# Root-mean-square norms: sums in four column tiles of PE, root and reciprocal on a quarter of the columns, spread back into PSUM by four products

## The reference

```python
def rms_norm(x, g):
    y = xf * lax.rsqrt(jnp.mean(xf * xf, axis=-1, keepdims=True) + RMS_EPS)
    return (y * g.astype(jnp.float32)).astype(x.dtype)
...
a_lat = modulate(rms_norm(h_lat, g_pre_t), sh_t, sc_t)      # before the mixer
h_lat = h_lat + gt_t * rms_norm(y_lat, g_post_t)            # residual behind it
f_lat_in = modulate(rms_norm(h_lat, g_pre_f), sh_f, sc_f)   # before the channels
h_lat = h_lat + gt_f * rms_norm(f_lat, g_post_f)            # residual behind them
```

## Time and profile before

| | |
|---|---|
| median of 3 runs | 2568.89 us (2568.54 to 2573.36) |
| the profiled execution | 2565.24 us, its span 2563.4 us |
| PE busy | 2413.9 us, 94% of the span |
| DVE busy | 1755.0 us, 68% |
| ACT busy | 1385.1 us, 54% |
| mean granted PE clock | 0.968 |

### The profile page before, as it was taken

The page is one execution under the profiler, slowest core; times in us unless marked ns, Lnnn a source line. Parts: engine busy times, 40 slices in busy tenths (PEclk is TensorE's granted clock), DMA queues, the critical chain, the costliest instruction groups (busy, mean ns, idle before and its releaser), DMA issues.

```text
span 2563.4 us, 32159 instructions
## 1 busy us (share of the span) xinstructions
PE 2413.9 (94%) x12058; PEld 1946.4 (76%) x12058; DVE 1755.0 (68%) x1806; ACT 1385.1 (54%) x1455; POOL 46.1 (2%) x87
## 2 busy tenths in 40 slices
PE   6989999998999997877988999999999999999997
PEld 3757778875787884756886788888888888888886
DVE  3569753426333334778655989898889888888886
ACT  3366343333222222565545677777777777777775
POOL 0001000001000000000000000000000000000000
PEclk8989999999999998988998999999999999999998
DMA  7245223345434333313462889999999999989894
GB/s 269 76 131 186 66 91 105 109 157 190 139 107 140 99 100 114 99 42 103 148 236 99 335 351 368 351 366 350 367 342 369 356 361 352 364 343 373 339 373 178
DMA packets 104679, 579.36 MB, mean 226 GB/s; under 512 B 11920, under 2 KB 13840, under 8 KB 54800
## 3 DMA queue, kind: packets, MB, share of 16 engines
q1 hardware_dynamic: 93072, 536.21, 56.8%
q0 software_dynamic: 11520, 41.95, 4.7%
HBM read 577.06 MB, written 1.05 MB: 226 GB/s over the span
## 4 chain that ended last, share of the span: by engine, by line
PE 85%; DVE 9%; ACT 3%; issue 1%; DMA 1%; SPq 0%; DVEq 0%; ACTq 0%
PE bank L616 25%; PE bank L618 25%; PE bank L617 25%; DVE cacc L1534 2%; PE bank L679 2%; PE bank L986 1%; PE bank L778 1%; DVE rstd L1475 1%; PE bank L1051 1%; PE bank L798 1%; DVE t L1490 1%; PE bank L654 1%; DVE al L1496 1%; DVE wlo L1455 1%; DMA mod_s<-in_mod 1%
## 5 line engine op out<-in xcount | busy, mean ns | idle before, releaser
L1756 DVE TENSOR_TENSOR elo<-eraw,ehi 128x2048 fp32r<-128x2048 f32 x388 | 884.9, 2287 | 136.3 <-ACT ehi L1143 135.1
L1143 ACT CAST ehi<-eraw 128x2048 fp32r<-128x2048 f32 x388 | 741.3, 1914 | 253.7 <-PE bank L618 249.8
L1455 DVE TENSOR_TENSOR wlo<-raw,whi 128x1024 fp32r<-128x1024 f32 x220 | 269.5, 1225 | 309.8 <-ACT whi L1099 308.0
L616 PE MATMUL bank<-ah,whi 128*128 128x512 f32 (+1 forms) x1088 | 399.9, 368 | 23.9 <-DVE al L1496 15.6
L616 PE MATMUL bank<-ehi,xgh 128*128 128x512 f32 x1024 | 405.8, 396 | 1.5 <-DVE xgl L1762 1.2
L617 PE MATMUL bank<-elo,xgh 128*128 128x512 f32 x1024 | 399.6, 390 | 0.0
L618 PE MATMUL bank<-ehi,xgl 128*128 128x512 f32 x1024 | 399.4, 390 | 0.0
L617 PE MATMUL bank<-al,whi 128*128 128x512 f32 (+1 forms) x1088 | 391.1, 359 | 0.0
L618 PE MATMUL bank<-ah,wlo 128*128 128x512 f32 (+1 forms) x1088 | 390.9, 359 | 0.0
L1099 ACT CAST whi<-raw 128x1024 fp32r<-128x1024 f32 x220 | 229.2, 1042 | 129.4 <-PE bank L618 117.3
L616 PEld LDWEIGHTS bank<-ah,whi 128*128 128x128 f32 x1088 | 208.3, 191 | 70.3 <-DVE al L1496 17.5
(11 more groups left out here) (270 smaller groups left out, 2778.7 us busy)
## 6 DMA issues: line engine op xcount, KB each, us to landing
eraw<-in_moe SPq DMA_DIRECT2D x388, 1024.0 KB, 4.9
raw<-in_dense SPq DMA_DIRECT2D x220, 512.0 KB, 3.5
mod_b<-in_mod POOLq DMA_DIRECT2D x48, 512.0 KB, 5.3
mod_a<-in_mod POOLq DMA_DIRECT2D x32, 512.0 KB, 4.2
mod_s<-in_mod SPq DMA_DIRECT2D x16, 512.0 KB, 12.9
hres<-in_xT SPq DMA_DIRECT2D x1, 2048.0 KB, 8.1
wsT<-in_wsT SPq DMA_DIRECT2D x2, 512.0 KB, 3.6
out_h<-hres SPq DMA_DIRECT2D x2, 512.0 KB, 3.0
```

Of the source, the lines that this page charges most:

```text
L616: pe.matmul(dst, wh, xh, start=first, stop=False, skip_group_check=True)
L1143: nc.scalar.copy(ehi[c % ESPLIT][:], eraw[c % ERAW][:]).then_inc(e_hi, 1)
L1455: dve.tensor_tensor(wlo[c % SPLIT][:], raw[c % RAW][:], whi[c % SPLIT][:].bitcast(F32), ALU.subtract).then_inc(w_lo, 1)
L1756: dve.tensor_tensor(elo[c % ESPLIT][:], eraw[c % ERAW][:], ehi[c % ESPLIT][:].bitcast(F32), ALU.subtract).then_inc(e_lo, 1)
```

## The change

In the seven norms the sum is made in quarters. `add_squares` multiplies the first 32 columns of `ones` by a quarter of the tokens for each of PE's four column tiles; quarter j of the sums then stands in partitions 32j to 32j + 31 of `STAT`, in columns 0 to 127 (64 for 256 tokens). Root and reciprocal run on these 128 (64) columns. `spread_roots` then brings quarter j to all partitions: a product whose weights are column 2j of `sel8` (one at partition 32j, zero elsewhere), repeated 128 times, writes it into columns of the PSUM bank `RB` (bank 7). DVE reads the factor from `RB` where it read `rstd`. The places of the new waits on PE's list: before layer 0 after chunk 12 of 16; at the residuals of layer 0 after five of eight chunks; otherwise right behind the sums.

```diff
+        RB = ps[7]
...
+            def add_squares(x, ntok, first, last):
+                w = ntok // 4
+                for j in range(4):
+                    mm = pe.matmul(STAT[32 * j:32 * j + 32, 0:w], ones[:, 0:32], x[:, j * w:(j + 1) * w],
+                                   start=first, stop=last, skip_group_check=True)
+                return mm
+
+            def spread_roots(ntok):
+                w = ntok // 4
+                pe.wait_ge(rs_ready, n.next(rs_ready))
+                for j in range(4):
+                    mm = pe.matmul(RB[:, j * w:(j + 1) * w], sel8[:, 2 * j:2 * j + 1].broadcast_to([P, P]),
+                                   rstd[:, 0:w], start=True, stop=True, skip_group_check=True)
+                mm.then_inc(rb_psum, 1)
...
                         for k in range(KD):
                             mod_chunk()
+                            if (v, k) == (1, 3):
+                                spread_roots(TOK)
                         if v == 0:
                             pe.wait_ge(ones_landed, 16)
-                            sum_squares(KD, lambda k: t16[:, k, :], TOK)
+                            sum_squares(KD, lambda k: t16[:, k, :], TOK, quarters=True)
                             turn_rows(0)
...
                     for k in range(KD):
                         mod_chunk()
+                        if k == KD // 2:
+                            spread_roots(TOK)
                     stat_bank()
                     for k in range(KD):
                         pe.wait_ge(sq_ready, n.next(sq_ready))
-                        mm = pe.matmul(STAT[:], ones[:], t16[:, k, :], start=(k == 0), stop=(k == KD - 1),
-                                       skip_group_check=True)
+                        mm = add_squares(t16[:, k, :], TOK, k == 0, k == KD - 1)
                         if k == KD - 1:
                             mm.then_inc(sumsq_psum, 1)
                         mod_chunk()
                     n.next(sumsq_psum)
+                    spread_roots(TOK)
...
                     if f >= 1:
                         pe.wait_ge(sq_ready, n.next(sq_ready))
-                        pe.matmul(STAT[:, 0:nq], ones[:], ysq[:, (f - 1) % 2, 0:nq], start=(f == 1), stop=False,
-                                  skip_group_check=True).then_inc(ysq_used, 1)
+                        add_squares(ysq[:, (f - 1) % 2, 0:nq], nq, f == 1, False).then_inc(ysq_used, 1)
...
                 else:
-                    sum_squares(KD, lambda k: t16[:, k, 0:nq], nq)
+                    spread_roots(nq)
+                    sum_squares(KD, lambda k: t16[:, k, 0:nq], nq, quarters=True)
+                    spread_roots(nq)
...
+            def root_quarters(ntok):
+                w = ntok // 4
+                act.wait_ge(sumsq_psum, n.next(sumsq_psum))
+                nc.scalar.activation(std[:, 0:w], STAT[:, 0:w], ACT.Sqrt, bias=eps[:, 0:1], scale=1.0 / D
+                                     ).then_inc(std_ready, 1)
...
+            def invert_quarters(ntok):
+                dve.wait_ge(std_ready, n.next(std_ready))
+                dve.reciprocal(rstd[:, 0:ntok // 4], std[:, 0:ntok // 4]).then_inc(rs_ready, 1)
+                dve.wait_ge(rb_psum, n.next(rb_psum))
...
                             dve.scalar_tensor_tensor(t16[:, k, lo:hi], hres[:, k, lo:hi],
-                                                     modc[:, 2 * which, s, k:k + 1], rstd[:, lo:hi],
+                                                     modc[:, 2 * which, s, k:k + 1], RB[:, lo:hi],
                                                      ALU.mult, ALU.mult).then_inc(norm_t, 1)
...
-                    chain(dve.tensor_tensor(y[:, k, 0:ntok], y[:, k, 0:ntok], rstd[:, 0:ntok], ALU.mult))
+                    chain(dve.tensor_tensor(y[:, k, 0:ntok], y[:, k, 0:ntok], RB[:, 0:ntok], ALU.mult))
```

More of the change, by code:

```diff
@@ L405, in build @@
         std_ready = sem("std_ready")
+        rs_ready = sem("rs_ready")
+        rb_psum = sem("rb_psum")
         rdiag_ready = sem("rdiag_ready")
@@ L647, in stat_bank, with sum_squares @@
                     pe.wait_ge(std_ready, n.n[sumsq_psum])
-            def sum_squares(nk, src, ntok):
-                stat_bank()
+            def add_squares(x, ntok, first, last):
[11 more added lines that the diff above has]
+                mm.then_inc(rb_psum, 1)
+            def sum_squares(nk, src, ntok, quarters=False):
+                stat_bank()
+                if quarters:
+                    for k in range(nk):
+                        pe.wait_ge(sq_ready, n.next(sq_ready))
+                        mm = add_squares(src(k), ntok, k == 0, k == nk - 1)
+                    mm.then_inc(sumsq_psum, 1)
+                    n.next(sumsq_psum)
+                    return
                 for k in range(nk):
@@ L895, in _ @@
                         pe.wait_ge(sq_ready, n.next(sq_ready))
-                        pe.matmul(STAT[:, 0:nq], ones[:], ysq[:, (f - 1) % 2, 0:nq], start=(f == 1), stop=False,
-                                  skip_group_check=True).then_inc(ysq_used, 1)
+                        add_squares(ysq[:, (f - 1) % 2, 0:nq], nq, f == 1, False).then_inc(ysq_used, 1)
                 pe.wait_ge(sq_ready, n.next(sq_ready))
-                pe.matmul(STAT[:, 0:nq], ones[:], ysq[:, 1, 0:nq], start=False, stop=True,
-                          skip_group_check=True).then_inc(sumsq_psum, 1)
+                add_squares(ysq[:, 1, 0:nq], nq, False, True).then_inc(sumsq_psum, 1)
                 n.next(sumsq_psum)
@@ L939, in _ @@
                                 pe.wait_ge(sq_ready, n.next(sq_ready))
-                                pe.matmul(STAT[:], ones[:], fh[:, (f - 1) % 2, :], start=(f == 1), stop=False,
-                                          skip_group_check=True).then_inc(ysq_used, 1)
+                                add_squares(fh[:, (f - 1) % 2, :], TOK, f == 1, False).then_inc(ysq_used, 1)
                         k0 += ng
                     pe.wait_ge(sq_ready, n.next(sq_ready))
-                    pe.matmul(STAT[:], ones[:], fh[:, 1, :], start=False, stop=True,
-                              skip_group_check=True).then_inc(sumsq_psum, 1)
+                    add_squares(fh[:, 1, :], TOK, False, True).then_inc(sumsq_psum, 1)
                     n.next(sumsq_psum)
@@ L1159, in _ @@
                     copy_rows(0)
-                    root(TOK, 1.0 / D, 0)
+                    root_quarters(TOK)
                     copy_rows(1)
@@ L1328, in _ @@
                 n.next(ysq_used, 1)
-                root(nq, 1.0 / D, 0)
+                root_quarters(nq)
                 if L:
@@ L1560, in _ @@
                 nq = live(L)
-                invert(TOK)
+                invert_quarters(TOK)
                 if L == 0:
@@ L1723, in _ @@
                     rest_to(CHUNK[("out", L, f)] + 2)
-                invert(nq)
+                invert_quarters(nq)
                 residual(0, nq, y16)
-                invert(nq)
+                invert_quarters(nq)
                 if L == 0:
```

## The result

The change makes the kernel faster: 2546.28 us (median of 6 runs, 2544.56 to 2550.53) against 2568.59 (6 runs, 2565.36 to 2573.36), a ratio of 0.9914, 95% interval 0.9901 to 0.9926, or 22.3 us. The forecast of 2552.0 had 16.9 us of gain; its range, 2544 to 2563, holds the time.

What follows compares the result with a forecast made beforehand. PE held 85% of the chain, nearly all untouched dense products, so only stretches around seven norms could gain. Terms 0.8 + 2.6 - 1.3 + 3.0 + 3.9 + 7.9 + 0.2 - 0.2 = 16.9 us gave 2552.0, range 2544 to 2563.

Steps and rivals of the forecast that it cites:

- Reciprocal and root: In the seven norms: shorter columns save 2.72 us per 512-column norm and 1.36 per 256-column one.
- The spread: Four fp32 products behind each reciprocal take 1.15 us at the high clock, 2.1 at the low one.
- The sum product in quarters: Each narrow sum product on PE takes 0.33 us, 0.65 at the low clock, weight loading setting the pace.
- Changing tile size: Among dense products, 0.31 us to narrow tiles and back; saves 0.22 a product in layer 0, loses 0.21 in layer 1.
- Start: Norm before layer 0: shorter first sums, but chunks wait for their loads; gain 0.8 us.
- First norms: Behind layer 0's output and down projections, DVE starts 1.5 us earlier each, 3.0 us together.
- Second norm, layer 0: DVE leads instead of PE, so modulated tiles start earlier; 3.9 us beyond the 1.5 already counted.
- Ahead of layer 1: Run of sum products and chunks takes 9.0 us, not 15.3; with the norm, a gain of 7.9 us.
- PSUM operand: DVE's residual products read the factor from PSUM instead of SBUF; priced at nothing.
- The clock did not stay low around the norms: Rival: PE's clock stays low around the norms, leaving a gain of 6.1 us, 2563; chance 15%.
- The dear PSUM operand: Rival: 80 DVE instructions reading PSUM cost 76 ns more each, 6 us lost, 2558; chance 7%.
- The rival with streaming alone and a clock that rises at once: Narrow products cost only streaming, or size changes are cheaper, and the clock rises at once: 23 to 25 us, 2545; chance 12%.

Runs made afterwards that it cites:

- second pair: Second profiled executions of the unchanged kernel before and of the unchanged changed kernel; 2565.10 us and 2546.14 us.
- the double sums: Changed kernel with every narrow sum product inside a dense stream issued twice; 2552.70 us, 0.9941 of the kernel before.
- the version with both edits: Changed kernel with layer 1's 256-token norms put back and, ahead of layer 1, modulation chunks behind the sums; median 2541.92 us over 11 runs.

## Why the prediction was right, point by point

- **Bound.** Right in that the change gains around the norms alone, and that DVE took PE's place behind layer 0's output projection. But stretches that it does not touch moved too: the part ahead of layer 0's output projection, layer 1's attention, and in the second pair t4 to a, by 2.6.
- **Reciprocal and root.** 953 ns against 0.95 us, root 0.38 against 0.37. Right.
- **The spread.** 1.15 us taken, 1.17 measured at the high clock. At the low one 2.1 taken, 2.06 in the start and 1.97 on layer 1's second norm; its first took 1.59, in part at the low clock, so that the 0.2 that I had it gain became a loss of 0.3 (from the root's start to DVE's first tile 2.59 us, before 2.30). The timeline:

```profile
1357.94 1.59 PE L665 MATMUL bank<-rstd,sel 128*128 128x64 f32 x8 [1.90 <-DVE rstd L1517]
...
1368.42 1.97 PE L665 MATMUL bank<-rstd,sel 128*128 128x64 f32 x8 [1.02 <-DVE rstd L1517]
```

- **The sum product in quarters: the term that was mis-sized.** I took 0.33 us at the high clock, with weight loads setting the pace; it is 0.22, and 0.43 at the low one (0.65 taken). That is a quarter of the full product's 0.86, streaming and nothing else, my lower end. The line through 64- and 128-column loads did not hold for 32 columns: their eight loads hide behind the streaming. That makes a pair of product and chunk 0.65 us and not 0.78. The rule of the Trainium skill, TensorE: Matmul & The Clock Gate, Part 3, that tiles of different column groups start about 4 ns apart, agrees with the trace: four tiles one after the other on PE's list take 0.22 us, a quarter of 0.86.
- **Changing tile size.** 0.31 taken, 0.34 measured (0.56 - 0.22), and the double sums show that it is paid once for a group. The product among dense ones costs 0.56, not 0.64; by the time from one to the next the gain is 0.31 a tile, 12 x 0.31 = 3.7 us, not 2.6. In layer 1 a 64-column product is 0.11 us, not the 0.33 that I had kept for it, and the predicted loss of 1.3 did not come: the stage is 0.1 worse.
- **Start.** +0.8 taken; the first modulated tile came at 34.05, before at 34.54: +0.5, and +0.3 in the second pair. The sums took 1.93 us, not 4, and it did not matter, since the chunks behind waited for their loads. Another 1.0 came by 60 us in the first profile, as the dense products found the high clock earlier (0.87 from 34 to 60 us, before 0.74). That was luck: in the second profile of the change the clock there is 0.74 as before, and the 1.0 is not there.
- **First norms.** 1.5 each taken, 1.5 measured twice: the table load gave nothing, five chunks hid root and reciprocal.
- **Second norm, layer 0.** DVE leads, as said. 3.9 taken, 4.6 and 4.2 measured: the last product was 0.47 behind the square, and the spread took 1.17 in the first profile and 1.58, in part at the low clock, in the second.
- **Ahead of layer 1.** 7.9 taken, 9.9 and 9.1 measured: 6.9 us from product to root, and 7.8 in the second profile, not 9.0. A pair is 0.65 and not 0.78 (1.28 and not 1.54 at the low clock), and the low clock lasted 4.0 us and 5.6, not 6. My own terms, 6 + 4.1 x 0.78 less the last chunk, add up to 8.75 and not 9.0.
- **PSUM operand.** Nothing taken, nothing found.
- **The rivals.** The clock did not stay low around the norms. The dear PSUM operand is refuted, and with it here the section on the TRN2 errata in the Trainium skill, VectorE: DVE Perf Modes, by which PSUM would cost more than SBUF: the rows differ by 3 ns the other way. A narrow product above 1.58 us among dense ones would have decided for slower: it is 0.56. The rival with streaming alone and a clock that rises at once, 2545, was nearest. Its price of the product was right; the clock ahead of layer 1 did not rise at once. That its time is so near is in part the 4.7 us that the attention took back.
- **What I left out.** A stage without one changed instruction moved by 4.7 us, more than most terms of the sum. The two errors have opposite signs, so that the total was off by only 5.7 us is in part luck: the norms gave 20 to 22 us where I had 16.9, the code ahead of the output projection 1.2 to 1.8 where I had nothing, and the attention took 4.7.

## What to carry to other kernels

A sum over partitions by a product with `ones` writes the same number into 128 partitions; given to four column tiles it costs a quarter, even in fp32 with a weight load for each, and leaves the result in the shape in which root and reciprocal are short too. It pays most where PE is late in an alternating run; next to full-width products each change of size and back costs a third of a microsecond, so narrow products should stand together. Judge such a change by stages between shared landmarks: a stage that it does not touch may shift by more than its terms (here one did by 4.7 us, and one varied by 7.5 with no edit in it), and a total then says little about a 2 us edit.

## What the runs showed of the hardware

- Layer 1's attention, 520 products on PE in a chain with DVE and ACT, took from 97.5 to 107.8 us in 14 profiles (with the part of the gated MLP behind it), its mean granted clock from 0.90 to 0.82. The length goes with how long before the entry the clock had fallen to 0.50 (1.2 GHz): 1.1 to 1.3 us gave 102.2 to 102.3 in five profiles, 2.2 gave 97.5 in three. Two profiles of before and two of the change agreed to 0.1 us, two of the version with both edits did not (97.5, 101.0).
- The rest behind MAX8, 46% of the program, took 1166.1 to 1167.2 us in all kernels that are compared there, whenever it was entered.
- ACT's root of 32 partitions takes as long as one of 128: 0.36 us for 128 columns, four of them 1.47.
- Four column tiles of 128 x 32 in fp32 take exactly a quarter of the full product, 0.22 for 0.86, down to 64 columns each (0.11).
